# Half the frequencies of a token transform, a 280-column projection, and a memory-query chunk placed earlier

## What is computed

```python
def _fourier_mix(f, w_f):
    bn, L, _ = f.shape
    fh = f.reshape(bn, L, FNET_HEADS, FNET_HEAD_DIM).astype(jnp.float32)
    spec = jnp.fft.fft2(fh, axes=(1, 3), norm="ortho").real
    return spec.astype(f.dtype).reshape(bn, L, FNET_WIDTH) @ w_f
...
    yc = _fourier_mix(f_in, fnet_w) * jax.nn.silu(f_gate)
...
        proj = hn @ w_in[l]
        conv_a, conv_b, q, k_c, v_c, k_s, v_s, k_w, v_w, gate_logits = jnp.split(proj, IN_SPLITS, axis=-1)
...
        h = h + memory_attention(rmsnorm(h, mem_q_norm_g[l]), rmsnorm(mem, mem_kv_norm_g[l]),
                                 w_mem_q[l], w_mem_k[l], w_mem_v[l], w_mem_o[l])
        h = h + peer(rmsnorm(h, peer_norm_g[l]), peer_w_q[l], peer_sub_keys[l], peer_u[l], peer_v[l])
```

## Time and profile before

| | |
|---|---|
| median of 3 runs | 2675.55 us (2675.37 to 2677.31) |
| profiled execution | 2673.3 us, span 2671.4 us |
| TensorE matmuls | 2374.0 us busy, 89% |
| VectorE | 1432.6 us, 54% |
| ScalarE | 682.5 us, 26% |
| GpSimd | 611.7 us, 23% |
| DMA | 657.20 MB, mean 246 GB/s |
| mean granted TensorE clock | 0.96 |

### The profile page before, as it was taken

The page is one execution under the profiler, slowest core; times in us unless marked ns, Lnnn a source line. Parts: engine busy times, 40 slices in busy tenths (PEclk is TensorE's granted clock), DMA queues, the critical chain, the costliest instruction groups (busy, mean ns, idle before and its releaser), DMA issues.

```text
span 2671.4 us, 23577 instructions
## 1 busy us (share of the span) xinstructions
PE 2374.0 (89%) x7882; PEld 1247.0 (47%) x7882; DVE 1432.6 (54%) x3726; ACT 682.5 (26%) x1640; POOL 611.7 (23%) x566
## 2 busy tenths in 40 slices
PE   6999999989999999899989898888888878788776
PEld 2456554444645456448845444444334334343332
DVE  0010222026532667521577777787777777677765
ACT  2000012015511124512234222233222232222222
POOL 0002000001000000000144444444444444344441
PEclk9999999989999989899999999999999999899999
DMA  8101332000021110013299999999999999999996
GB/s 332 63 32 67 154 138 114 32 32 1 5 98 63 67 64 32 33 63 126 98 400 397 421 421 421 421 413 422 421 422 421 422 420 421 422 421 421 421 421 276
DMA packets 83943, 657.20 MB, mean 246 GB/s; under 512 B 9410, under 2 KB 9698, under 8 KB 11378
## 3 DMA queue, kind: packets, MB, share of 16 engines
q0 software_dynamic: 75760, 549.06, 49.7%
q1 hardware_dynamic: 8066, 106.65, 10.2%
HBM read 653.58 MB, written 2.10 MB: 245 GB/s over the span
## 4 chain that ended last, share of the span: by engine, by line
PE 56%; DMA 31%; DVE 9%; issue 2%; ACT 2%; POOL 0%; SPq 0%; DVEq 0%; POOLq 0%; PEldq 0%; ACTq 0%
DMA arena<-in_peer_uv,newton 29%; PE psum L573 21%; PE psum L1182 11%; PE psum L643 3%; DMA arena<-in_weights 2%; PE psum L1059 2%; DVE arena L2242 2%; PE psum L623 1%; PE psum L1124 1%; PE psum L1151 1%; PE psum L739 1%; PE psum L789 1%; PE psum L995 1%; PE psum L797 1%; PE psum L810 1%
## 5 line engine op out<-in xcount | busy, mean ns | idle before, releaser
L1182 PE MATMUL psum<-arena 128*128 128x512 f32 x2048 | 975.5, 625 | 205.6 <-ACT arena L1578 203.1
L2242 DVE CUSTOM_DVE_ANT_0 arena<-arena 128x1024 f32<-128x1024 f32 x512 | 620.8, 1224 | 284.7 <-DMA arena<-in_peer_uv,newton 280.8
L2400 POOL DMA_INDIRECT arena<-in_peer_uv,newton x512 | 569.3, 1112 | 835.6 <-PE psum L1182 708.3
L1182 PEld LDWEIGHTS psum<-arena 128*128 128x128 f32 x2048 | 397.4, 200 | 694.8 <-issue 690.2
L573 PE MATMUL psum<-arena 128*128 128x512 f32 (+2 forms) x1440 | 548.7, 542 | 10.9 <-DVE arena L1758 3.6
L573 PEld LDWEIGHTS psum<-arena 128*128 128x128 f32 (+1 forms) x1440 | 270.1, 189 | 287.2 <-issue 275.6
L1267 ACT ACTIVATE arena<-psum 128x512 f32<-128x512 f32 (+9 forms) x328 | 169.5, 535 | 696.8 <-PE psum L573 308.5
L1578 ACT ACTIVATE arena<-ident,newton 128x128 f32<-128x128 f32 x512 | 177.8, 394 | 266.9 <-DVE newton L2251 263.4
L1569 ACT ACTIVATE arena<-arena 128x2 f32<-128x2 f32 (+1 forms) x258 | 52.5, 203 | 660.5 <-DVE arena L2242 660.5
L1151 PE MATMUL psum<-arena 128*128 128x256 f32 x480 | 122.3, 380 | 0.9 <-DMA arena<-in_weights 0.4
L1151 PEld LDWEIGHTS psum<-arena 128*128 128x128 f32 x480 | 91.0, 190 | 62.5 <-issue 54.7
(11 more groups left out here) (307 smaller groups left out, 2086.4 us busy)
## 6 DMA issues: line engine op xcount, KB each, us to landing
arena<-in_weights SPq DMA_DIRECT2D x48, 2048.0 KB, 9.0
arena<-in_peer_uv,newton POOLq DMA_INDIRECT x512, 24.7
arena<-in_xin SPq DMA_DIRECT2D x1, 3072.0 KB, 28.5
arena<-in_dft_l POOLq DMA_DIRECT2D x1, 2048.0 KB, 16.3
arena<-in_cmp_w POOLq DMA_DIRECT2D x1, 2048.0 KB, 7.7
out<-arena SPq DMA_DIRECT2D x4, 512.0 KB, 11.8
arena<-in_pool_band POOLq DMA_DIRECT2D x1, 1280.0 KB, 12.7
arena<-in_fnet_w POOLq DMA_DIRECT2D x1, 1024.0 KB, 23.1
```

The costliest lines, as they stand in the source:

```text
L1182: ins = mm(bank(j_y[t][q]), DIAG[i % 4], ROW[ROW_PLACE[i]][:, D + 512 * q:D + 512 * q + 512], start=first, stop=last)
L2242: v.tensor_tensor_reduce(out=u, in0=u, in1=HNT[ITEM_TILE[i // 16]][:, :], scale=1.0, scalar=0.0, op0=ALU.mult, op1=ALU.add, accum_out=DOTS ...
L2400: g.indirect_dma_start(out=ROW[ROW_PLACE[i]][:, :], out_offset=None, in_=a["peer_uv"], in_offset=bass.IndirectOffsetOnAxis(ap=IDX[:, n, e: ...
```

## The change

It does three things. The token transform computes the frequencies 0 to 256 (`HL` is 256, so `HL + 1` columns); the products of line 746 then run twice, over columns 0 to 256 with the weights as they are, and over columns 1 to 255 with weights whose channels are mirrored inside each head, and DVE reads the second result backwards into the tokens 257 to 511. `DFTL` shrinks to 257 columns, `FNETW` grows to two sets, its area moves, and its load waits for the two chunk sums `j_ln_ab[0]`. The last projection block holds its 280 used columns in four pieces of 70, and line 888 reads only these. Chunk 4 of the memory queries of half 1 is computed between the chunk sum and the first query, in bank 5; ACT copies it behind the root of the norm.

```diff
--- before.py
+++ after.py
@@ -198,8 +198,8 @@
         VT = area(136, 6, 512)
         F_IN = area(96, 4, L)
         FAB = area(104, 4, 4, 256)
-        DFTL = area(120, 2, 4, L)
-        FNETW = area(136, 4, 512)
+        DFTL = area(120, 2, 4, HL + 1)
+        FNETW = area(128.25, 2, 4, 512)
         SPEC = area(72, 4, L)
         FG = area(148, 4, L)
         DG = area(156, 4, L)
@@ -217,7 +217,7 @@
         PTB = [area(kb, T) for kb in (86, 89, 92, 164)]
         RSQ = area(92, L)
         RSKV = area(80, T)
-        LSQ = area(144, T)
+        LSQ = area(145, T)
         CQSQ = [area(171, L), area(193, L)]
         RROT = area(195, 32)
 
@@ -486,11 +486,12 @@
         j_rms_pe = J.turn(1)
         j_mo = [J.turn(8, [j_rms_pe[0][0]])]
 
+        j_mq[1] += [J.take(5)]
         j_pq0 = [J.take(4), J.take(6)]
         j_sc0 = [J.take(1), J.take(2)]
         j_tx = [[J.take(k) for k in (0, 3, 5, 7)]]
         j_th = [[J.take(k) for k in (4, 6, 0, 3)]]
-        j_mq[1] += [J.take(k) for k in (5, 7, 5, 7)]
+        j_mq[1] += [J.take(k) for k in (7, 5, 7)]
         j_pq = [None, J.take(4)]
         j_sc = [None, J.take(2)]
         j_y = [[J.take(2 * (t % 2)), J.take(2 * (t % 2) + 1)] for t in range(4)]
@@ -736,14 +737,17 @@
                 claim(pe, j_dft2[h])
                 for t in range(4):
                     for q in range(2):
-                        ins = mm(bank(j_dft2[h]), FAB[:, t, h, q * P:(q + 1) * P], DFTL[:, q, t, :],
+                        ins = mm(bank(j_dft2[h], HL + 1), FAB[:, t, h, q * P:(q + 1) * P], DFTL[:, q, t, :],
                                  start=(t == 0 and q == 0), stop=(t == 3 and q == 1))
                 done(ins, j_dft2[h])
             read_out(pe, j_dft2)
             for m in range(4):
                 claim(pe, j_fnet[m])
                 for k in range(4):
-                    ins = mm(bank(j_fnet[m]), FNETW[:, k, m * P:(m + 1) * P], SPEC[:, k, :], start=(k == 0), stop=(k == 3))
+                    mm(bank(j_fnet[m], HL + 1), FNETW[:, 0, k, m * P:(m + 1) * P], SPEC[:, k, 0:HL + 1], start=(k == 0), stop=(k == 3))
+                for k in range(4):
+                    ins = mm(bank(j_fnet[m], HL - 1, HL + 1), FNETW[:, 1, k, m * P:(m + 1) * P], SPEC[:, k, 1:HL],
+                             start=(k == 0), stop=(k == 3))
                 done(ins, j_fnet[m])
 
             read_out(pe, j_kr)
@@ -885,7 +889,7 @@
                 j = j_v2[t]
                 claim(pe, j)
                 for k in range(KC):
-                    ins = mm(bank(j, 384), H[:, k, t * P:(t + 1) * P], w[:, 0:3, k, :], start=(k == 0), stop=(k == KC - 1))
+                    ins = mm(bank(j, 280), H[:, k, t * P:(t + 1) * P], w[:, :, k, 0:70], start=(k == 0), stop=(k == KC - 1))
                 done(ins, j)
             release_block(j)
 
@@ -1130,6 +1134,7 @@
 
             mem_o_step(0, 0, 8 * KC)
             chunk_sum(j_rms_pe[0], SUMA[:, :], HL, 40)
+            memory_queries(1, 4)
 
             def token_major(job, src, m0, t):
                 claim(pe, job)
@@ -1244,7 +1249,7 @@
                 token_major(j_tx[0][m], X, 4 * (m % 2), m // 2)
             for m in range(4):
                 token_major(j_th[0][m], HA, 4 * (m % 2), m // 2)
-            for c in range(4, 8):
+            for c in range(5, 8):
                 memory_queries(1, c)
             query_steps(1, 0, 2 * KC)
             key_scores(1)
@@ -1361,7 +1366,7 @@
                 t, hp = divmod(n, 2)
                 copy_out(j_dft1[n], FAB[:, t, 2 * hp:2 * hp + 2, :].rearrange("p a b -> p (a b)"))
             for h in range(4):
-                copy_out(j_dft2[h], SPEC[:, h, :])
+                copy_out(j_dft2[h], SPEC[:, h, 0:HL + 1], HL + 1)
             full(act, j_fnet[3])
             for h in range(8):
                 copy_out(j_qup[h], QT[0:QK, h, :], p1=QK)
@@ -1548,6 +1553,7 @@
                 read_out(act, [j_mo[0][k]])
                 fn(SQA[:, k, :], X[:, k, 0:HL], ACT.Square).then_inc(S["squared"], 1)
             root(j_rms_pe[0], RSA[:, :], HL)
+            memory_queries_out(1, 4)
 
             def query_out(hp):
                 copy_out(j_pq[hp], PQ[:, 2 * (hp % 2):2 * (hp % 2) + 2, :].rearrange("p a b -> p (a b)"))
@@ -1627,7 +1633,7 @@
             for m in range(4):
                 copy_out(j_th[0][m], HNT[m // 2][:, 512 * (m % 2):512 * (m % 2) + 512])
             topk_exp(0)
-            for c in range(4, 7):
+            for c in range(5, 7):
                 memory_queries_out(1, c)
             topk_exp(1)
             memory_queries_out(1, 7)
@@ -1877,7 +1883,8 @@
             for m in range(4):
                 j = j_fnet[m]
                 full(dve, j)
-                freed(v.tensor_tensor(FG[:, m, :], bank(j), FG[:, m, :], ALU.mult), j)
+                v.tensor_tensor(FG[:, m, 0:HL + 1], bank(j, HL + 1), FG[:, m, 0:HL + 1], ALU.mult)
+                freed(v.tensor_tensor(FG[:, m, HL + 1:L], bank(j, HL - 1, HL + 1)[:, ::-1], FG[:, m, HL + 1:L], ALU.mult), j)
 
             dve.wait_ge(S["mla_const_loaded"], 48)
             j = j_krr[0]
@@ -2346,7 +2353,9 @@
             full(pool, j_ab_out[14])
             full(pool, j_ab_out[15])
             load(flat3(DFTL[:, :, :, :]), "dft_l", "fft_const_loaded")
-            load(flat2(FNETW[:, :, :]), "fnet_w", "fft_const_loaded")
+            for s in range(2):
+                full(pool, j_ln_ab[0][s])
+            load(flat3(FNETW[:, :, :, :]), "fnet_w", "fft_const_loaded")
             pool.wait_ge(S["h_ready"], 16)
             pool.dma_start(MEMT, a["mem"].rearrange("p (k m) -> p k m", k=KC)).then_inc(S["mem_loaded"], 16)
 
@@ -2430,7 +2439,7 @@
     ac = 2 * np.pi * (np.outer(np.arange(P), np.arange(P)) % P) / P
     al = 2 * np.pi * (np.outer(t, t) % L) / L
     dft_c = np.concatenate([np.cos(ac), -np.sin(ac)], axis=1) / np.sqrt(L * P)
-    dft_l = np.stack([np.cos(al), np.sin(al)]).reshape(2, 4, P, L).transpose(2, 0, 1, 3)
+    dft_l = np.stack([np.cos(al), np.sin(al)])[:, :, 0:HL + 1].reshape(2, 4, P, HL + 1).transpose(2, 0, 1, 3)
     inv = (np.float32(10000.0) ** (-np.arange(0, 16, 2, dtype=f) / 16)).astype(f)
     rope = np.zeros((P, 2, L), f)
     swap = np.zeros((P, 32), f)
@@ -2471,6 +2480,7 @@
     out2 = i["w_out_2"][0]
     q2 = np.concatenate([w2[:, 1024 + 64 * h:1088 + 64 * h] for h in heads], axis=1)
     kv2 = [w2[:, 1536 + P * n:1664 + P * n] for n in range(6)]
+    v2 = np.concatenate([kv2[3], kv2[5], w2[:, 2304:2328]], axis=1)
     mats = [
         i["ab_w_mod"][0][:, 0:2 * D],
         np.concatenate([ab[:, 0:512], ab[:, 1536:2048], ab[:, 512:1024], ab[:, 1024:1536], ab[:, 2048:2560]], axis=1),
@@ -2481,12 +2491,13 @@
         np.concatenate([pad(cd[:, 1024:1440], 512), cd[:, 0:512], cd[:, 512:1024], cd[:, 1440:1952]], axis=1),
         i["cd_w_out"][0], i["w_mem_k_2"][0][:, 0:512],
         np.concatenate([w2[:, 0:1024], q2, kv2[0], kv2[1], kv2[2], kv2[4],
-                        pad(np.concatenate([kv2[3], kv2[5], w2[:, 2304:2328]], axis=1), 512)], axis=1),
+                        *[pad(v2[:, 70 * n:70 * n + 70], P) for n in range(4)]], axis=1),
         i["w_mem_k_2"][0][:, 512:D], i["w_mem_v_2"][0][:, 0:512],
         np.concatenate([out2[0:512]] + [out2[512 + 64 * h:576 + 64 * h] for h in heads], axis=0),
         i["w_mem_v_2"][0][:, 512:D], i["w_mem_q_2"][0], i["w_mem_o_2"][0], i["peer_w_q_2"][0],
     ]
     kvup = i["cd_w_kv_up"][0].reshape(P, HEADS, 2, 64)
+    fnet, mirrored = i["cd_fnet_w"][0], (P - np.arange(P)) % P
     x, cx = i["x"][0], i["ctx"][0]
     tok = np.concatenate([x, cx], axis=0)
 
@@ -2519,7 +2530,7 @@
         "sgu_w": i["ab_sgu_w"][0].transpose(2, 0, 1).reshape(P, -1),
         "w_q_up": rows_of(i["cd_w_q_up"][0], 2),
         "w_kv_up": kvup.transpose(0, 2, 1, 3).reshape(P, D),
-        "fnet_w": rows_of(i["cd_fnet_w"][0], 4),
+        "fnet_w": np.concatenate([rows_of(w, 4) for w in (fnet, fnet.reshape(4, P, -1)[:, mirrored].reshape(fnet.shape))], axis=1),
         "cmp_w1": i["cmp_w1_2"][0].reshape(2, 16, P, P).transpose(2, 0, 1, 3).reshape(P, -1),
         "cmp_w2": i["cmp_w2_2"][0].transpose(1, 0, 2).reshape(P, -1),
         "cmp_pos": i["cmp_pos_2"][0].reshape(2, 16, P).transpose(2, 0, 1).reshape(P, -1),
```

## The result

The changed kernel takes **2647.45 us** (median of 4 runs, 2642.77 to 2651.39); the kernel before, run beside it, 2676.01. The profiled execution took 2651.39 us, span 2649.5: by the two traces only 21.9 us are gone.

A forecast was written before the change was run, and what follows sets the result against it. TensorE's chain was taken to bound the first half, gather bytes the end; -13.7 - 0.2 - 5.8 - 3.3 = -23.0 us takes the median from 2675.55 to 2652.5 us, range 2648 to 2660.

The forecast's parts named there:

- The bound: Whole kernel: TensorE's chain bounds the first half, gather bytes the end from about 1360 us; first-half savings count by earlier gathers.
- Transform, line 739: Token transform: 64 records at 257 columns take 16.8 us instead of 30.52, so -13.7 us.
- Projection: Line 746, behind the token transform: 64 narrower records take 13.8 us where 32 took 13.9, so 0 us.
- the open loads: Rival at line 746: 32 added weight loads stand in the open, 6.1 us more, 2658.6 us; 3 in 100.
- the odd widths: Rival at lines 739 and 746: 257 and 255 columns cost as a full 512, 2680.1 us, slower; 3 in 100.
- The rule of the Trainium skill against it: Line 746: weight loads overlap running matmuls only where row groups differ, so 32 added loads of 190 ns would stand open.
- Loads of the constants: GpSimd's table and weight loads beside a late weight block: same 3 MB, so 0 us, bounds -1.5 and +1.
- 280 columns: Line 888, four token tiles: 0.236 us a record, 7.55 us for each two tiles, -5.8 us in whole.
- DVE's wait: DVE idle ahead of line 959 after its rotary products: 8.4 us of 12.5 are left, so TensorE stays last.
- Chunk: Memory-query chunk moved ahead of the first query: fills TensorE's gap, gathers run earlier, -3.3 us, bounds -1.2 and -4.6.
- The rival in which the clock falls all the same: At the moved chunk: clock falls although the gap is filled, about nothing left of that gain, 2655.8 us; 12 in 100.
- the spread: Allowance in the range for scatter of the runs: 1.4 us, up to 2660 us.

## Why the prediction was right or wrong

**The bound was right.** The first half was shortened and the gathers came earlier by what the first half lost: first gather -20.8, end -21.9.

**Transform, line 739: right.** 16.8 us forecast, 16.05 measured; with the copy (0.40 against 0.60) and the projection -13.8 in the mean of the traces, against -13.9. At 554 to 556 us the clock was 0.50, and it rose in the two windows after:

```profile
554.00:556.00 2.00, 2.00 (x6) 1.54 (x6) 0.00 (x0) 0.00 (x0) 0.00 (x0) 0.50 0.03 8
556.00:558.00 2.00, 2.00 (x8) 1.68 (x7) 0.00 (x0) 0.00 (x0) 0.00 (x0) 0.72 0.00 0
558.00:560.00 2.00, 2.00 (x11) 1.73 (x10) 0.00 (x0) 0.39 (x1) 0.00 (x0) 1.00 0.00 0
```

**Projection: right**, 14.05 us for 64 records against 13.8. The rivals of the open loads (6.1 us more) and of the odd widths (0.433 a record) are both refuted by the same rows: 0.215 us a record with its load inside. The rule of the Trainium skill against it (TensorE: Matmul & The Clock Gate, Part 3, The mechanism) does not hold for these loads; the measurement decides. The same section also has loads run ahead when they go to a background weight buffer, which would fit, but no run here shows where a load goes. The product read backwards cost 0.41 us beside 0.43 for the one read forwards, and delayed nothing.

**Loads of the constants: the step that failed.** It was put at 0, "as full while the block comes", with -1.5 as the bound. Bytes were compared, and not the rows in which they come. The change has the same 3 MB, but rows of half the length beside the block: it lands 1.4 to 2.1 us sooner after its request than the 11.7 of the old loads, and to the transform's start that is -2.0 us, below the bound's end. The loads split in two (1.1 us) show the cause of the larger part.

**280 columns: right**: 0.236 a record as interpolated, -5.55 us in the traces and -6.5 (interval -2.9 to -8.3) by the runs, for -5.8. DVE's wait is 8.81 for 8.4.

**Chunk: right in size.** Forecast -3.3, traces -3.3, runs -4.35 (-1.3 to -7.2). The clock stayed, the first 48 records took 6.49 for 6.3, and GpSimd no longer stops ahead of row 4. The rival in which the clock falls all the same is refuted.

**The sum and its range.** With the loads' term the traces give -15.6 - 5.55 - 3.3 = -24.45 us. Measured were -28.6 (interval -24.4 to -33.5) and -31.6 (-26.0 to -33.7). So of the 5.6 us that were missed by the first of these, 1.4 are in the terms (2.0 for the loads, the others 0.6 smaller than forecast); for the other 4.2 the traces show no step. The second failed step is **the spread**: one trace of before was taken as if its clock were the kernel's, and 1.4 us were given for the runs. But stretches that the change doesn't touch take 2, 3.3, 3.5 and 4 us more or less from one execution to the next, and the gather up to 4: before's single runs reach from 2668 to 2682 us over the studies, and the difference of two traces was 21.9 us where the medians differ by 28.6. A range of 4.5 us below the forecast was too narrow for a median of four. Chance does not cover all of it, though: the nine runs of the changed kernel have a mean of 2646.3 us, 30.5 below the 2676.8 of all 64 runs of the kernel before, within 2.4 by their scatter. The account's 24.45, itself good to some 1.5 us, lies outside of that. So a few us of the gain have no place in it, and their cause stays open.

## What to carry to other kernels

Price matmuls by the chain's length over its count, for each width, and the forecast of a narrower product held here to some per cent, odd widths and pieces included, where TensorE was last. When a load is changed, look not only at its bytes but at the length of its rows and at what urgent load shares the engines with it; asking for it after the urgent one took the rest of the wait away, here under 1 us. Before a difference of some us is explained, compare several traces stage by stage: stages that the change doesn't touch show how much comes from the clock and from the gather's start alone, and the range should be at least that wide. And when several comparisons all err to one side, put their runs together before calling it chance.

## What was not expected of the hardware

Behind a row of 32 one-column records the granted clock was 0.50 although PE was busy without a break, and the sum behind it took 9.68 or 8.67 us instead of 6.9. The same records laid between wide ones cost 0.34 us for four and left the clock at 1.00. A weight block of 2 MB landed 1.1 us earlier when the neighbouring 2 MB came in rows of 8 KB instead of 16 (10.62 against 11.62 to 11.81).
